# Bias rows laid out on the host, and six modulation blocks multiplied around the end of the odd input projection

## The reference, cut to what matters

```python
def ada_modulation(cond, w_mod, b_mod):           # both layers: 1024 -> 6*1024
    m = jax.nn.silu(cond) @ w_mod + b_mod
    return jnp.split(m, N_MOD, axis=-1)           # sh1, sc1, g1, sh2, sc2, g2

# even layer
h  = modulate(rms_norm(x, norm_mix), sh1, sc1) @ w_in     # -> Fourier part, q, k, v
# neighbourhood attention of the latent tokens:
bias  = rpb[:, dr_idx][:, :, dc_idx]                       # relative position, 8 heads
s_loc = jnp.where(mask, q @ k.T * scale + bias, NEG_INF)
x = x + g1 * (concat(fourier, attention) @ w_out)
x = x + g2 * swiglu(modulate(rms_norm(x, norm_ffn), sh2, sc2), w1, w3, w2)
# odd layer
h = modulate(rms_norm(x, norm_mix), sh1, sc1) @ w_in       # -> q, k, v, S5 input
x = x + g1 * (concat(grouped attention, S5) @ w_out)
x = x + g2 * moe_swiglu(modulate(rms_norm(x, norm_ffn), sh2, sc2), router, experts)
```

## Time and profile before

| | us |
|---|---|
| three runs, median (lowest to highest) | 1909.77 (1906.45 to 1913.3) |
| the profiled execution | 1914.57 |
| its span | 1912.7 |
| TensorE busy | 1814.9 (95%) |
| VectorE, ScalarE, POOL busy | 1265.6, 1003.7, 312.3 |
| granted TensorE clock, mean | 0.977 |

### The profile page before, as it was taken

How to read it: one execution, slowest core, us unless ns; L and a number is a source line. 1 busy time by engine, 2 the same in 40 slices (tenths; PEclk the granted TensorE clock), 3 DMA queues, 4 the chain that set the end, 5 groups by cost and what they waited for, 6 DMA issues and landing times.

```text
span 1912.7 us, 25247 instructions
## 1 busy us (share of the span) xinstructions
PE 1814.9 (95%) x8938; PEld 1413.6 (74%) x8938; DVE 1265.6 (66%) x1329; ACT 1003.7 (52%) x1096; POOL 312.3 (16%) x584
## 2 busy tenths in 40 slices
PE   4999788999999989797999999999999999999998
PEld 2666444888888876465888888888888888888886
DVE  3243734442433234744998989989889898898997
ACT  3222423421312121363677767777777777776774
POOL 6887931011111124101000000000000000000000
PEclk8999899999999999897999999999999999999999
DMA  9788532122323151502799999999989999898994
GB/s 371 307 337 272 195 127 88 43 111 77 121 77 121 45 203 56 165 2 88 289 370 355 352 370 337 368 352 355 371 344 359 349 358 368 346 362 345 364 367 182
DMA packets 72374, 481.55 MB, mean 252 GB/s; under 512 B 8368, under 2 KB 11568, under 8 KB 17456
## 3 DMA queue, kind: packets, MB, share of 16 engines
q1 hardware_dynamic: 68720, 470.82, 64.5%
q0 software_dynamic: 2448, 7.61, 1.5%
q10 hardware_dynamic: 1136, 2.21, 0.4%
HBM read 473.29 MB, written 7.32 MB: 251 GB/s over the span
## 4 chain that ended last, share of the span: by engine, by line
PE 90%; DMA 3%; DVE 3%; POOL 2%; issue 1%; ACT 1%; SPq 0%; DVEq 0%; ACTq 0%; POOLq 0%
PE bank L1042 32%; PE bank L1056 16%; PE bank L775 12%; PE bank L745 4%; PE bank L804 3%; PE bank L792 3%; PE bank L625 3%; PE bank L840 2%; DMA ring<-in_ev_mod 2%; PE bank L563 2%; PE bank L1015 2%; PE bank L1025 1%; PE bank L713 1%; PE bank L605 1%; PE bank L696 1%
## 5 line engine op out<-in xcount | busy, mean ns | idle before, releaser
L1806 DVE TENSOR_TENSOR rest<-ring,WR 128x2048 fp32r<-128x2048 f32 x336 | 758.3, 2288 | 80.6 <-ACT WR L1373 80.1
L1373 ACT ACTIVATE WR<-ring 128x2048 fp32r<-128x2048 f32 x336 | 632.3, 1917 | 48.4 <-DMA ring<-in_experts 47.9
L1042 PE MATMUL bank<-WR,xer 128*128 128x512 f32 x1792 | 582.0, 397 | 0.8 <-DVE s5v L1967 0.8
L1042 PEld LDWEIGHTS bank<-WR,xer 128*128 128x128 f32 x1792 | 337.0, 188 | 70.3 <-issue 0.8
L1042 PE MATMUL bank<-rest,xer 128*128 128x512 f32 x896 | 349.5, 390 | 0.0
L1056 PE MATMUL bank<-WR,heTr 128*128 128x512 f32 x896 | 282.2, 392 | 0.0
L775 PE MATMUL bank<-hTr,WR 128*128 128x512 f32 x672 | 207.2, 390 | 0.0
L1056 PEld LDWEIGHTS bank<-WR,heTr 128*128 128x128 f32 x896 | 168.2, 188 | 34.6
L1042 PEld LDWEIGHTS bank<-rest,xer 128*128 128x128 f32 x896 | 169.1, 189 | 32.9
L1056 PE MATMUL bank<-rest,heTr 128*128 128x512 f32 x448 | 174.4, 389 | 0.0
L1658 DVE TENSOR_TENSOR rest<-ring,WR 128x2048 fp32r<-128x2048 f32 (+2 forms) x38 | 80.3, 2115 | 123.9 <-ACT WR L1298 123.6
(11 more groups left out here) (338 smaller groups left out, 2175.4 us busy)
## 6 DMA issues: line engine op xcount, KB each, us to landing
ring<-in_experts SPq DMA_DIRECT2D x336, 1024.0 KB, 4.8
ring<-in_ev_mod SPq DMA_DIRECT2D x24, 1024.0 KB, 9.0
ring<-in_od_mod SPq DMA_DIRECT2D x24, 1024.0 KB, 8.6
ring<-in_ffn_up SPq DMA_DIRECT2D x22, 1024.0 KB, 6.8
ring<-in_ffn_down SPq DMA_DIRECT2D x12, 768.0 KB, 5.1
ring<-in_ev_in SPq DMA_DIRECT2D x8, 1024.0 KB, 6.7
ring<-in_ev_out SPq DMA_DIRECT2D x4, 1024.0 KB, 8.5
ring<-in_od_out SPq DMA_DIRECT2D x4, 1024.0 KB, 13.5
```

The lines of the kernel that those rows point to most:

```text
L1042: mm = pe.matmul(bank[m % 2][:, :], xer[:, i, 4 * kh + k, :], w[j][:, 512 * k:512 * k + 512], start=(kh == 0 and k == 0 and x == 0), stop= ...
L1373: act.activation(part(0, h), ring[:, h % HALVES, :], ACT.Copy).then_inc(split_hi, 1)
L1806: dve.tensor_tensor(part(1, h), ring[:, h % HALVES, :], part(0, h).bitcast(F32), ALU.subtract).then_inc(split_lo, 1)
```

## The change

The bias table is expanded on the host to one 128 x 512 block per head, and SP loads a bias with one DMA into one of three buffers. The group of blocks 12 to 23 becomes two groups, 12 to 17 and 18 to 23. The second is loaded behind the odd projection's weights and multiplied into bank 6: blocks 18 and 19 behind jobs 8 and 9 of the odd projection, 20 behind job 11, 21 and 22 in `turn_odd`, 23 in step 2 of the odd attention. The conditioning vector for them is loaded again and goes through Silu again on ScalarE. The odd projection's jobs 10 and 11 use other banks.

```diff
-         + [("in", 0), ("mod", 4), ("mod", 5), ("mod", 6), ("in", 1), ... ("in", 3)]
-         + [("mod", s) for s in range(14, 24)])
-UNDER_IN = {(0, 2): 4, (0, 3): 5, (0, 5): 6, (0, 7): 7, (5, 2): 8, (5, 7): 9, (7, 4): 10, (8, 7): 11, (9, 5): 12,
-            (10, 2): 13, (12, 0): 14, (13, 4): 15, (15, 0): 16}
-UNDER_TURN = {2: 17}
-UNDER_FOUR = {4: 18}
-UNDER_ATTN = {0: 19, 2: 20, 4: 21, 6: 22, 8: 23}
+         + [("in", 0), ("mod", 4), ("mod", 5), ("in", 1), ("mod", 6), ("mod", 7), ("mod", 8), ("in", 2),
+            ("mod", 9), ("mod", 10), ("mod", 11), ("in", 3)]
+         + [("mod", s) for s in range(12, 18)])
+UNDER_IN = {(0, 4): 4, (0, 6): 5, (4, 4): 6, (5, 5): 7, (6, 6): 8, (8, 3): 9, (9, 4): 10, (10, 4): 11, (12, 3): 12,
+            (13, 4): 13, (14, 4): 14, (15, 4): 15}
+UNDER_TURN = {1: 16}
+UNDER_FOUR = {}
+UNDER_ATTN = {1: 17}
-MOD_GROUPS = ((0, 4), (4, 12), (12, 24))
+MOD_GROUPS = ((0, 4), (4, 12), (12, 18), (18, 24))
+ODD_TURN = {0: 21, 3: 22}
+ODD_ATTN = {2: 23}
+ODD_IN = {8: 18, 9: 19, 11: 20}
+LATE_SLOT = [2, 0, 2, 0, 1, 1]
+ODD_BANK = (4, 5, 6, 7, 4, 5, 6, 7, 4, 5, 7, 4)
...
 # SP
+            def load_bias(h):
+                if h >= 3:
+                    sp.wait_ge(bias_ready, h - 2)
+                sp.dma_start(bias_raw[h % 3], a["rpb"][:, h]).then_inc(bias_landed[h % 3], 16)
+
             for i, (what, n) in enumerate(EARLY):
+                if i == S_MOD[12]:
+                    for h in range(3):
+                        load_bias(h)
+                if i == S_MOD[15]:
+                    for h in range(3, 5):
+                        load_bias(h)
                 load(i, ...)
             for n in range(2):
                 load(S_OUT_E + n, a["ev_out"][n])
+            for h in range(5, NA_HEADS):
+                load_bias(h)
...
             sp.dma_start(U, scr_u.rearrange("(a b) c -> a b c", b=CHUNK)).then_inc(u_landed, 16)
+            for n in range(5):
+                load(S_LATE + n, a["od_mod"][6 + n])
             sp.wait_ge(lag_ready, 1)
...
+            load(S_LATE + 5, a["od_mod"][11])
             for n in range(2):
                 load(S_OUT_O + n, a["od_out"][n])
 # PE, w_in_odd
-                        pe.wait_ge(*((in_copied, i + 5) if i < 8 else (in_normed, i + 1)))
+                        pe.wait_ge(*((in_copied, i + 5) if i < 8 else (in_normed, i + 1 if i < 10 else i + 2)))
+                    if i == 11:
+                        pe.wait_ge(in_copied, 13)
...
                     s5_between(i)
+                    if i in ODD_IN:
+                        if ODD_IN[i] == LATE:
+                            pe.wait_ge(late_ready, 1)
+                            pe.wait_ge(in_normed, 11)
+                        modulation(ODD_IN[i])
 # PE, turn_odd (behind the wait for lag_ready)
+                    if jj in ODD_TURN:
+                        modulation(ODD_TURN[jj])
 # PE, odd attention
+                        elif r in ODD_ATTN:
+                            modulation(ODD_ATTN[r])
+                        if steps is ODD_STEPS and r == ODD_ROW + 1:
+                            pe.wait_ge(in_normed, 15)
+                            modulation_turn(3)
 # ACT, ahead of modulate(1); and at u == 5 of the feed-forward part
+            act.dma_start(late_cond[0], a["late"][:, 0:252]).then_inc(late_landed, 16)
+            act.dma_start(late_cond[1], a["late"][:, 252:336]).then_inc(late_landed, 16)
...
+                    act.activation(late_cond[0], late_cond[0], ACT.Silu)
+                    act.activation(late_cond[1], late_cond[1], ACT.Silu).then_inc(late_ready, 1)
 # DVE
+                        if steps is ODD_STEPS and r == ODD_ROW:
+                            modulation_row(3)
+                        if r == ODD_ROW + 1:
+                            modulated(3, (3,))
-            modulated(2, (2, 3))
+            modulated(2, (2,))
 # POOL, head_bias
-                if h + 1 < NA_HEADS:
-                    if h >= 1:
-                        pool.wait_ge(bias_ready, h)
-                    load_bias(h + 1)
-                pool.wait_ge(bias_landed[h % 2], 64 * (h // 2 + 1))
+                pool.wait_ge(bias_landed[h % 3], 16 * (h // 3 + 1))
...
-                pool.tensor_tensor(b, raw[:, :, ::-1], cst[:, C_MASK:C_MASK + GRID_W].unsqueeze(1)
+                pool.tensor_tensor(b, raw, cst[:, C_MASK:C_MASK + GRID_W].unsqueeze(1)
...
-            load_bias(0)
             for h in range(2):
                 head_bias(h)
-            for k in range(8, 12):
+            for k in range(8, 13):
                 table(k)
-            head_bias(2)
-            head_bias(3)
-            for k in range(12, 16):
-                table(k)
-                head_bias(k - 8)
+            for h in range(2, NA_HEADS):
+                head_bias(h)
+                if h % 2 == 1:
+                    table(12 + h // 2)
```

More of the change, by code:

```diff
@@ L66 @@
 ROW_JOB = 9
-S_MOD = [EARLY.index(("mod", s)) for s in range(24)]
+S_MOD = [EARLY.index(("mod", s)) for s in range(18)]
 S_IN_E = [EARLY.index(("in", n)) for n in range(4)]
-MOD_GROUPS = ((0, 4), (4, 12), (12, 24))
-S_OUT_E, S_FFN = 28, 30
+MOD_GROUPS = ((0, 4), (4, 12), (12, 18), (18, 24))
+LATE = 18
+ODD_TURN = {0: 21, 3: 22}
[3 more added lines that the diff above has]
+ODD_BANK = (4, 5, 6, 7, 4, 5, 6, 7, 4, 5, 7, 4)
+ODD_ROW = max(ODD_ATTN) + 1
+S_OUT_E, S_FFN = 22, 24
 S_IN_O = S_FFN + UP_SLOTS + DOWN_SLOTS
-S_OUT_O = S_IN_O + 4
+S_LATE = S_IN_O + 4
+S_OUT_O = S_LATE + 6
+S_MOD += [S_LATE + n for n in range(6)]
 S_MOE = S_OUT_O + 2
@@ L212, in build @@
         silc = cond.rearrange("p (k s) -> p k s", s=62)
+        late_more = sb("late_more", [P, 84])
+        late_cond = [B[:, 11008:11260], late_more[:, :]]
+        silc_late = [x.rearrange("p (k s) -> p k s", s=42) for x in late_cond]
         hT = HT[:, :].rearrange("p (c t) -> p c t", c=DC)
@@ L228, in build @@
         bias = [S[:, at:at + 512] for at in (0, 512, 4608, 5120)]
-        bias_raw = B[:, 8192:9216].rearrange("p (b n) -> p b n", b=2)
+        bias_raw = [B[:, at:at + 512] for at in (8192, 8704, 10368)]
         prob = S[:, 1024:2560].rearrange("p (b n) -> p b n", b=3)
@@ L356, in part @@
             return (WR if i == 0 else rest)[:, h % HALVES, 0:n]
-        SLOTS = EARLY_SLOT + [i % RING for i in range(S_OUT_E, S_MOE)]
+        SLOTS = (EARLY_SLOT + [i % RING for i in range(S_OUT_E, S_LATE)] + LATE_SLOT
+                 + [i % RING for i in range(S_OUT_O, S_MOE)])
         def slot(i):
@@ L433, in mod_bank @@
         def mod_bank(g):
-            return bank[(0, 3, 7)[g]]
+            return bank[(0, 3, 7, 6)[g]]
         def mod_rows(g):
-            return (mrow[:, 0, :], mrow[:, 1, :], rows[:, 0:512])[g]
+            return (mrow[:, 0, :], mrow[:, 1, :], rows[:, 0:512], HT[:, 3072:3584])[g]
         def mod_turn_bank(g):
-            return ((bank[1], 0), (bank[3], 0), (bank[6], 0))[g]
+            return ((bank[1], 0), (bank[3], 0), (bank[6], 0), (bank[7], 0))[g]
         HALVES2 = (slice(0, HD), slice(HD, 2 * HD))
@@ L525, in expert_weights @@
                     if rnd == 0:
-                        sp.wait_ge(*read(S_MOE - RING + u // 2))
+                        sp.wait_ge(*read((S_LATE + 5, S_OUT_O, S_OUT_O + 1)[u // 2]))
                     expert_half(0, NE * rnd, u, rnd > 0)
@@ L562, in modulation @@
                         c = 4 * i + j
-                        mm = pe.matmul(o[32 * j:32 * j + 32, :], silc[:, c, at:at + 32], w[:, c, :],
+                        x = (silc[:, c, at:at + 32] if s < LATE else
+                             silc_late[c // 6][:, c % 6, at - 20:at + 12])
+                        mm = pe.matmul(o[32 * j:32 * j + 32, :], x, w[:, c, :],
                                        start=(s == lo and i == 0), stop=(s == hi - 1 and i == 1))
@@ L839, in w_in_odd @@
                     for c in range(DC):
-                        mm = pe.matmul(bank[4 + i % 4][:, 0:w_], hT[:, c, t * P:(t + 1) * P], w[:, c // 4, c % 4, :],
+                        mm = pe.matmul(bank[ODD_BANK[i]][:, 0:w_], hT[:, c, t * P:(t + 1) * P], w[:, c // 4, c % 4, :],
                                        start=(c == 0), stop=(c == DC - 1))
@@ L932, in s5_out @@
                     pe.wait_ge(t_landed, 16 * CHUNK)
+                    pe.wait_ge(mod_ready, 2)
                     pe.wait_ge(s5_prev, 2)
@@ L1348, in _ @@
                 act.wait_ge(in_psum, 16 + i + 1)
-                ps = bank[4 + i % 4]
+                ps = bank[ODD_BANK[i]]
                 if n == 0:
@@ L1783, in _ @@
                        qn[:, t, 512 * (n - 1):512 * (n - 1) + w_].rearrange("p (h d) -> p h d", d=HD))
-                dve.tensor_tensor(dst, bank[4 + i % 4][:, 0:w_].rearrange("p (h d) -> p h d", d=HD),
+                dve.tensor_tensor(dst, bank[ODD_BANK[4 + i]][:, 0:w_].rearrange("p (h d) -> p h d", d=HD),
                                   hss[:, 0:heads].unsqueeze(2).to_broadcast([P, heads, HD]),
@@ L2103, in _ @@
             pool.wait_ge(s5_raw, 32)
```

(20 more changed lines are left out.)

15 lines of the change are left out of this document (9 added, 6 removed).

## The result

| | before | after |
|---|---|---|
| median of the runs compared | 1910.14 us (20) | 1913.97 us (20; 1911.71 to 1920.57) |
| the profiled execution / its span | 1914.57 / 1912.7 | 1917.63 / 1915.4 |
| granted TensorE clock, mean | 0.977 | 0.978 |

A forecast was written before the change was run, and what follows sets the result against it. It took POOL to bound the even attention's latent half, and TensorE the even projection and Fourier part. From 1914.6 us, 22.7 early gain and 7.9 late cost gave 1899.8, 4.8 less for the median: 1895, range 1885 to 1905.

The forecast's parts named there:

- item 3: Even attention's latent half: eight steps of 3.95 us plus 3.6 give 35.2 for 47.2, gaining 12.0 (5 to 15.6).
- late sum: Odd projection and odd attention: six blocks coming in cost 7.9 us in all, between 4 and 17.
- block 23: Odd attention: lands at about 802 to 803, reached at about 802.6; costs 2.4 us, between 1.9 and 6.
- either this lateness or one collision: Latent half: 3.6 us added for late biases or one scaling colliding with POOL; bounds 0 and 11.
- The projection: Even projection: one block fewer (1.9 us) and three waits of TensorE gone (3.4); gain 5.3, at worst 1.9.
- one block fewer up to the scores: Turn and Fourier part before the even scores: two blocks become one, gaining between 1.4 and 1.9 us.
- Item 4: Context half of the even attention: a block, a bank copy and its turn leave; gain 3.5 us, bounds 1.5 and 5.
- A: Latent half: POOL not the bound, removing issues gives only the late bias; item 3 is 5, time 1902; chance 0.17.
- B: Both attentions: no collision and a warm clock; item 3 gives 15.6, late sum 4.5; -24, 1886; chance 0.11.
- C: Odd part: the ring's waits come back, up to 6.9 + 1.9 us a block; 1940; chance 0.07.
- D: Even attention: TensorE at 1.2 GHz throughout, latent half 53 us; 1919.5; chance 0.05.
- three signs of error: TensorE waits for od_mod above 3 us in the odd part, latent half above 42, or projection ending behind 162 us.

The follow-up runs named there:

- e5: e3 with tables 13 and 14 made ahead of bias 2 and table 15 behind the last bias: 1893.97 us, ratio 0.9905.
- e1: The kernel after, with SP's loads of biases 5 to 7 moved ahead of the even output projection's loads: 1911.95 us, ratio 1.001.
- e10: e5 with the loads of biases 5 to 7 back behind the even output projection's loads: 1901.87 us, ratio 0.995.
- e6: e3 with the arithmetic of tables 13 to 15 left out, their save kept: 1896.18 us, ratio 0.9914.
- e2: The kernel after, with block 23's load moved ahead of the lags' round trip on SP: 1903.2 us, ratio 0.9964.
- e8: e3 with blocks 18 to 23 cut to four instructions of 64 columns and loads of 64 columns: 1895.91 us, ratio 0.9914.
- e12: e5 with POOL waiting for its own last instruction after each bias and each of a table's first three multiplications: 1901.89 us, ratio 0.9953.
- e4: The kernel before, with only the biases laid out on the host; POOL issues one load a bias instead of four: 1903.2 us, ratio 0.9971.
- e9: e4 with tables 12 and 13 ahead of bias 2, 14 and 15 behind bias 7, no late blocks: 1899.05 us, ratio 0.9951.
- e3: The kernel after, with both biases 5 to 7 and block 23 loaded earlier, the edits of e1 and e2: 1903.36 us, ratio 0.9963.
- e7: e2 with bias loading, padded table and POOL's order as in the kernel before, so the late blocks alone: 1910.2 us, ratio 0.9994.
- e11: e3 with POOL waiting for its own last instruction after each bias and each of a table's first three multiplications: 1899.91 us, ratio 0.9949.

## Why the prediction was wrong

Every mechanism that it summed is there, and in e5 nearly at its size: the attention starts 7.8 us earlier (7.2 forecast), the latent half is 12.3 shorter (12.0), the context half 2.3 (3.5), together 22.3 for 22.7; the late blocks cost 4.7 of it for 7.9 (up to the odd output projection). But that is a kernel with other orders on SP and POOL. For the kernel as changed, the profiled execution came out at 1917.6 for 1899.8, 17.8 us too long, and two terms failed: item 3 (9.6 us of it) and the late sum's block 23 (about 6).

**Item 3, the 3.6 us "either this lateness or one collision".** Measured: 13.3 us above eight steps of 3.95. Step by step (additions at 178.76, 182.95, 188.21, 192.67, 196.90, 205.56, 214.09, 219.75): block 17 on a slow clock 1.3, late bias 4.7, collision 4.6, cold TensorE behind it 1.7, the rest 1.0. "Or" was the error, and the collision was priced without the slow clock behind it. Both delays come: e1 shows the collision without the late bias, e10 the late bias without tables 13 and 14 between the biases (a scaling of 3.05 us stays), e6 neither (33.6). In e1 the same piece of two biases and a table stalls VectorE though no bias is late, so it is the order of POOL's program that makes the piece. The arrival itself was off by 5 us: 196 forecast, and POOL used bias 5 at 201.18. Two of them are the first load of the output projection, issued at 185.57 for 183.6; the rest is that bias 5 came 15.6 us behind that issue, for some 12.4 in the forecast. The two slots ahead of it landed 14.9 us behind the issue, for 11 taken and a bound of 13.8, so the bound was too low as well.

**The late sum, block 23.** Block 23, the group's row and turn and the clock together were to cost 1.9 us behind the first odd scores; they cost 8.2. Of these 0.6 stay in e2, and 7.6 are block 23's wait and the slow clock behind it, which the forecast had at 0.5. The order was foreseen, the arrival was not. TensorE reached the block 7.5 us behind the first odd scores (793.2), as forecast (802.6 for scores at 795.2). But the load was issued 1.0 us behind these scores instead of 1.7 ahead of them, and from the issue at 786.73 to the multiplication at 799.01 it took 12.3 us, for 8.5 to 9.5.

The late issue has a cause that the forecast left out. The lags' save was issued at 775.98 and their first load, which waits for it, at 781.45: 5.5 us. Before, it was 2.0:

```profile
782.11 0.34 SPq L503 DMA_DIRECT2D scr_lag<-rows  x1
784.11 1.32 SPq L508 DMA_DIRECT2D rows<-scr_lag  x2
```

The save now stands behind block 22's 2 MB, issued at 772.99 and multiplied from 780.94. In e8, where these loads are cut to 64 columns, the same stretch is 2.1 us again (769.98 to 772.06), and in e2, with block 23's 2 MB ahead of the save as well, it is 8.1. What the DMA engines did while block 23 was on its way, after:

```profile
786.00:793.00 7.00, 3.93 (x20) 1.48 (x17) 5.49 (x16) 3.90 (x10) 0.00 (x0) 1.00 1.24 143
793.00:799.00 6.00, 0.20 (x2) 0.02 (x1) 3.68 (x9) 1.44 (x4) 0.00 (x0) 0.75 0.97 396
```

They are full in both windows, but move 143 GB/s in the first, with the lags' short rows, and 396 in the second. That the block waits behind those rows fits this, and e2, which loads it ahead of them, has no wait for it; the rows alone were not tried. The block then runs at 1.2 GHz (2.78 us for ten instructions that take 1.48).

**Right.** The projection (-5.3 at its end, exactly), one block fewer up to the scores (1.6 for 1.9), blocks 18 and 19 (3.6 for 3.8), blocks 20 to 22 (2.6 for 2.2), the first odd scores at 1.13 us. Block 15 behind SP's wait for the biases, named as doubtful, was harmless here and cost TensorE a wait of 4.5 us in e12.

**Item 4** gave 1.5 for 3.5, and 2.3 in e5 (the block that leaves the context half is 23, which the forecast calls 22). The trace shows a part: VectorE's sixteen scalings there take 9.21 us together, 7.97 before, beside POOL's powers (L2072 to L2077), and a step there takes 2.6 to 3.5 us. What else holds it was not tried. And the output projection's first 16 instructions, partly at 1.2 GHz before and after, take 9.65 us for 8.80.

**The rivals.** A said that POOL is not the bound and that removing its issues gives only the late bias, item 3 being 5. The first half is refuted: with POOL's tables moved or left out the latent half falls to 34.9 and 33.6. The second half came true in e4, where the issues went and the half fell by 4.8. It was POOL's tables between the biases, not its issues, that held VectorE, and the change left them there. A's 1902 also lay nearer. The sum of B is wrong by 2 us: its terms give 26.3 - 4.5 = 21.8 and 1888, not 24 and 1886. How the 12.7 in its "item 3 would be 12.7 to 14" comes about is not worked out. C (waits for the ring) came true for one block of six: 5.8 us. D (the clock) was taken for all or nothing. The granted clock of the latent half is 0.89 before and 0.81 after, not by the steps' own gaps, as D had it, but behind each stall; e9, without a long stall, has 1.00 (the latent half of after, columns as above).

```profile
178.00:224.00 46.00, 30.76 (x215) 18.26 (x213) 35.96 (x75) 20.54 (x47) 27.58 (x51) 0.81 0.44 174
```

On this, "TensorE: Matmul & The Clock Gate" of the Trainium skill (section "Part 1: The HAM clock gate") has the array drop to 1.2 GHz when idle; the 1.97 and 1.98 us behind waits of 5.7 and 3.9 us agree.

Two of the three signs of error that the prediction names appeared: the latent half above 42 us (44.9) and waits of TensorE for od_mod above 3 us in the odd part (6.9).

## What to carry to other kernels

When two delays can both come, add them, and add what the slower clock costs the engine that idles behind them. A small transfer that an engine waits for goes ahead of the large ones in its queue, even if it is needed later; and a small transfer that others wait for (the lags' save) is slow behind a large one. Before work is moved off an engine, ask whether its remaining work can be moved into its own idle time: here two tables moved gave some 9 us (e3 to e5), more than the whole change with its queue repaired (7.1, e3).

## What the runs showed of the hardware

A SBUF-to-SBUF scaling on VectorE (0.49 us alone) that meets POOL at work is held up. In most meetings it waited only for the POOL instruction that was running and took 0.7 to 1.5 us. At times it was held over several: 4.83 to 5.19 us where POOL ran two biases and four multiplications without a pause (after, e1, e2, e3, e8), 2.63 us behind two biases alone (e5), 3.05 to 4.17 in others (before, e4, e7, e10), and at most 1.91 where POOL paused after each instruction (e11). Which of the two it will be was not found. The bias additions and the reductions on a bank kept their usual length beside POOL (0.42 and 0.69 us, 0.43 and 0.69 at the longest in all the traces of the latent half). "SBUF — State Buffer" of the Trainium skill (section "SBUF: two separate sides") has the holder of the shared ports keep them for its whole instruction. The short holdups agree with this. The long ones do not, and there the measurement decides: POOL kept them from one instruction to the next, and a pause of about 0.1 us was enough to pass them on.

Small transfers came late behind large ones of their queue. 256 KB behind 4 MB came to use 13.5 us after their issue (after); 2 MB behind the lags' eight loads were multiplied 12.3 us after theirs, for 6.91 alone; 5.5 us passed from the lags' save, behind 2 MB, to the issue that waits for it, for 2.0 before and 2.1 in e8.
